# Attention of block 1: scores with the keys on partitions, and sums from a column of ones beside V

## The reference, cut to what matters

```python
def blocked_gqa(q, k, v):
    ...
    def one_block(qi):
        s = jnp.einsum("bqgrd,bkgd->bgrqk", qi, k)
        p = jax.nn.softmax(s, axis=-1)
        return jnp.einsum("bgrqk,bkgd->bqgrd", p, v)
```

## Time and profile before

| | |
|---|---|
| median of 3 runs | 2699.52 us (2699.20 to 2699.63) |
| span of the profiled execution | 2697.8 us |
| TensorE busy with matmuls | 2665.9 us (99%), 13860 records |
| TensorE loading stationary operands | 2195.1 us (81%) |
| DVE busy | 1526.9 us (57%) |
| ACT busy | 1173.5 us (43%) |

### The profile page before, as it was taken

One profiled execution on the slowest core, in us unless ns is written; L12 is line 12 of the kernel. 1 busy time (PEld: TensorE's weight loads), 2 busy tenths in 40 slices (PEclk: granted clock), 3 DMA queues, 4 the chain that ended last, 5 costly groups with the idle time before them and its releaser, 6 DMA issues.

```text
span 2697.8 us, 33846 instructions
## 1 busy us (share of the span) xinstructions
PE 2665.9 (99%) x13860; PEld 2195.1 (81%) x13860; DVE 1526.9 (57%) x2142; ACT 1173.5 (43%) x1732; POOL 26.8 (1%) x45
## 2 busy tenths in 40 slices
PE   9989999999989999999999999999999999999998
PEld 8777888888777888888888888888777888888887
DVE  7885444345885444344444356899978844544433
ACT  6784332225784322233322234455688452432221
POOL 0000000000000000000000000000000000000000
PEclk9999999999999999999999999999999999999999
DMA  6303333324303333333333342222223432333332
GB/s 216 94 2 110 100 96 95 98 83 148 94 2 110 102 94 97 97 94 97 100 94 96 98 138 86 72 74 76 77 86 96 133 94 94 98 98 94 98 94 67
DMA packets 75801, 255.55 MB, mean 95 GB/s; under 512 B 9088, under 2 KB 12288, under 8 KB 75264
## 3 DMA queue, kind: packets, MB, share of 16 engines
q1 hardware_dynamic: 73136, 240.29, 29.3%
q0 software_dynamic: 2512, 13.11, 1.3%
HBM read 241.30 MB, written 8.39 MB: 93 GB/s over the span
## 4 chain that ended last, share of the span: by engine, by line
PE 93%; DVE 4%; ACT 3%; issue 1%; DVEq 0%; ACTq 0%
PE PS L1469 27%; PE PS L1471 27%; PE PS L1470 27%; PE PS L1719 1%; PE PS L1701 1%; PE PS L1428 1%; PE PS L1488 1%; PE PS L1487 1%; PE PS L1489 1%; DVE WLO L2216 0%; PE PS L1665 0%; ACT WHI L1805 0%; PE PS L1537 0%; PE PS L1535 0%; PE PS L1539 0%
## 5 line engine op out<-in xcount | busy, mean ns | idle before, releaser
L1469 PE MATMUL PS<-HHI,WHI 128*128 128x512 f32 x2256 | 893.2, 396 | 0.0
L1471 PE MATMUL PS<-HHI,WLO 128*128 128x512 f32 x2256 | 878.8, 390 | 0.0
L1470 PE MATMUL PS<-HLO,WHI 128*128 128x512 f32 x2256 | 878.3, 389 | 0.0
L2216 DVE TENSOR_TENSOR WLO<-WR,WHI 128x1024 fp32r<-128x1024 f32 (+2 forms) x450 | 535.0, 1191 | 495.4 <-ACT WHI L1805 492.2
L1805 ACT CAST WHI<-WR 128x1024 fp32r<-128x1024 f32 (+2 forms) x450 | 457.5, 1018 | 445.6 <-PE PS L1471 421.9
L1469 PEld LDWEIGHTS PS<-HHI,WHI 128*128 128x128 f32 x2256 | 423.6, 188 | 92.1 <-issue 4.8
L1470 PEld LDWEIGHTS PS<-HLO,WHI 128*128 128x128 f32 x2256 | 423.7, 188 | 89.9 <-issue 4.1
L1471 PEld LDWEIGHTS PS<-HHI,WLO 128*128 128x128 f32 x2256 | 423.4, 188 | 88.8
L1469 PE MATMUL PS<-FHI,WHI 128*128 128x512 f32 x682 | 265.3, 389 | 0.0
L1470 PE MATMUL PS<-FLO,WHI 128*128 128x512 f32 x682 | 265.3, 389 | 0.0
L1471 PE MATMUL PS<-FHI,WLO 128*128 128x512 f32 x682 | 265.3, 389 | 0.0
(11 more groups left out here) (381 smaller groups left out, 2727.5 us busy)
## 6 DMA issues: line engine op xcount, KB each, us to landing
WR<-in_stream SPq DMA_DIRECT2D x402, 512.0 KB, 3.6
WR<-in_stream SPq DMA_DIRECT2D x32, 384.0 KB, 3.0
xkeep<-X POOLq DMA_DIRECT2D x3, 2048.0 KB, 9.4
X<-xkeep POOLq DMA_DIRECT2D x24, 256.0 KB, 4.7
WR<-in_stream SPq DMA_DIRECT2D x16, 328.0 KB, 4.0
ROT<-RQ SPq DMA_DIRECT2D x40, 64.0 KB, 2.0
X<-in_xin SPq DMA_DIRECT2D x8, 256.0 KB, 4.9
out<-X SPq DMA_DIRECT2D x8, 256.0 KB, 2.2
```

The costliest lines, as they stand in the source:

```text
L1469: e.matmul(out, hi[:, i, :], xhi, start=first, stop=False)
L1470: e.matmul(out, hi[:, i, :], xlo, start=False, stop=False)
L1471: t = e.matmul(out, lo[:, i, :], xhi, start=False, stop=final)
L2216: e.tensor_tensor(lo, raw, hi.bitcast(F32), ALU.subtract).then_inc(S["dve_low"], 1)
```

## The change

In each layer the attention is computed per head instead of per pair and chunk.
- **Maxima first.** `maxima` adds, for each pair m and each c, a step `qk` of two matmuls, one per head, on the 64 partitions that hold that head's high part (every fourth query, `c::CH`), against 64 partitions of `KDS[0]`. `max` reduces the result to the negated maximum, `NM`. No low part takes part, and nothing else is done with these scores.
- **The maximum as a row.** Per head two DMAs on SP's queue, `qdup` (the head's high part to `QM`, 64 rows) and `mrow` (the four columns of `NM` to row 64 of `QM`). On POOL two memsets write the ones: row 64 of `KDS[1]`, and column 64 of V's two groups.
- **Scores with keys on partitions.** `ks`, 4 steps per head: for 128 keys, `KDS[0]` stationary and the query tile moving, then `KDS[1]` (65 rows) stationary and `QM` moving: 512 queries along the free axis, the maximum already subtracted. `exp` writes the exponentials straight to a tile `PTS`; there is no `accum_out`, `nrm`, `prs`, `pT` or `pta`.
- **PV with the probabilities stationary.** `pv`, one step per head: for each chunk of 128 queries and each of 4 key blocks a single-precision matmul, 128x128 exponentials stationary, 65 moving columns of V (the last one gives the sum). `yn` (DVE) divides.
- **Back to channels.** `hT`, one step per pair: four PE transposes, then `yv` on whole tiles of 512.
- **Plan.** The pauses `pace1` and `pace2` become 0.1, and `TIMES` has new entries. `kdup` has three DMAs instead of four.

```diff
@@ -152,7 +152,7 @@
...
-    "qk": (("pe", 0.92),), "qhi": (("act", 0.76785),), "qlo": (("dve", 1.3),), "pT": (("pe", 0.45),), "pv": (("pe", 0.95),),
+    "qk": (("pe", 0.25),), "ks": (("pe", 0.46),), "mrow": (("sp", 0.3),), "qdup": (("sp", 0.1),), "qhi": (("act", 0.76785),), "qlo": (("dve", 1.3),), "hT": (("pe", 0.45),), "pv": (("pe", 1.9),),
...
+    "max": (("dve", 0.7),), "yn": (("dve", 0.75),), "yv": (("act", 0.62), ("dve", 0.7),),
...
+DELAY = {"v": 0.38043, "zsilu": 0.77358, "pace1": 0.1, "pace2": 0.1, "turned": 0.81963, "sums": 0.30369, "ss": 1.401,
+         "hsum": 0.075925, "picked": 0.55886, "lru": 5.6906, "sq": 0.27228, "third": 0.17664, "merged": 0.20081, "until": 0.087442, "row": 2.6}
@@ -198,8 +198,10 @@
-PR_OF = [i % 3 if i < 8 else (3, 4, 2, 0, 1)[(i - 8) % 5] for i in range(4 * NH)]
-PR_BEFORE = {i: max(k for k in range(i) if PR_OF[k] == PR_OF[i]) for i in range(4 * NH) if PR_OF[i] in PR_OF[:i]}
+TILES = NH * CH
+EARLY = 24
+PT_OF = [i % 5 if i < EARLY else (4, 5, 6, 7, 8, 0, 1, 2)[i - EARLY] for i in range(TILES)]
+PT_BEFORE = {i: max(k for k in range(i) if PT_OF[k] == PT_OF[i]) for i in range(TILES) if PT_OF[i] in PT_OF[:i]}
@@ -595,61 +597,68 @@
             yield from self.added(("rope", l, t - 1))
         self.add("rcs", l, t)
 
...
+    def maxima(self, l, m):
+
+        for c in range(CH):
+            yield from self.room(2)
+            while self.tokens_wait:
+                yield 0.1
+            for h in (2 * m, 2 * m + 1):
+                self.take(("qk", l, h, c), "side")
+            yield self.add("qk", l, m, c)
+            for h in (2 * m, 2 * m + 1):
+                last = self.add("max", l, h, c)
+                self.free(("qk", l, h, c), ("dve_max", last))
+            yield self.pace
+        yield last
+        for h in (2 * m, 2 * m + 1):
+            self.spawn(self.head(l, h))
+
+    def head(self, l, h):
+
+        if h > 0:
+            yield from self.added(("ks", l, h - 1, CH - 1))
+        if h >= 2:
+            yield from self.until(("ks", l, h - 2, CH - 1))
+        self.add("qdup", l, h)
+        self.add("mrow", l, h)
+        yield DELAY["row"]
+        for k in range(CH):
+            i = CH * h + k
+            if i in PT_BEFORE:
+                yield from self.added(("pv", l, PT_BEFORE[i] // CH))
+            if PT_OF[i] >= 5:
+                yield from self.added(("qlo", l, 4))
+            yield from self.room()
+            while self.tokens_wait:
+                yield 0.1
+            self.take(("ks", l, h, k), "side")
+            yield self.add("ks", l, h, k)
+            exp = self.add("exp", l, i)
+            self.free(("ks", l, h, k), ("act_exp", exp))
+            yield self.pace
         yield exp
...
+        if h > 0:
+            yield from self.added(("yn", l, h - 1))
         yield from self.room()
...
+        self.take(("pv", l, h), "side")
+        yield self.add("pv", l, h)
+        done = self.add("yn", l, h)
+        self.free(("pv", l, h), ("dve_yn", done))
+        if h % 2:
+            yield done
+            yield from self.room()
+            self.take(("hT", l, h // 2), "side")
+            yield self.add("hT", l, h // 2)
+            self.free(("hT", l, h // 2), ("dve_yv", self.add("yv", l, h // 2)))
 
     def attention(self, l):
         yield from self.until(("v", l))
...
+        for m in range(NH // 2):
+            yield from self.until(("kdup", l), ("qlo", l, 1 + m))
+            if m > 0:
+                yield from self.added(("qk", l, m - 1, CH - 1))
+            self.spawn(self.maxima(l, m))
 
     def conv(self, l, j):
         if j > 0:
@@ -1234,12 +1243,12 @@
-    V = sb("V", 192, [CH, P])
-    PR = sb("PR", 194, [2, T])
-    PT = sb("PT", 198, [2, 2, CH, P])
-    NM = sb("NM", 206, [8])
-    RSM = sb("RSM", 206.0625, [8])
-    RIN = sb("RIN", 206.125, [8])
+    V = sb("V", 192, [CH, 2, 65])
+    PT = sb("PT", 194.03125, [5, T])
+    QM = (sb("QM", 76, [T], F32R), sb("QM2", 204.03125, [T], F32R))
+    NM = sb("NM", 206.03125, [NH, CH], F32R)
+    RIN = sb("RIN", 206.1875, [2, CH])
+    YVS = (sb("YV", 180, [4, T]), sb("YV2", 207.5, [4, T]))
...
+    PTS = [PT[:, i, :] for i in range(5)] + [RQ[:, i, :] for i in range(4)]
@@ -1356,6 +1366,10 @@
+    def heads_tokens(m):
+        return YVS[m // 2][:, 2 * m % 4, :].rearrange("p (c x) -> p c x", c=CH)
@@ -1676,31 +1690,40 @@
                 transposes(step, [Z[:, c, i * P:(i + 1) * P] for c in range(CH)]).then_inc(S["pe_turn"], 1)
 
             elif kind == "qk":
...
+                l, m, c = a
+                q.wait_ge(s_keys, 48 * (l + 1))
                 q.wait_ge(S["dve_qlow"], n["qlo", l, 1 + m])
...
+                for i, half in enumerate((slice(0, 64), slice(64, P))):
+                    emptied(q, ("qk", l, 2 * m + i, c))
+                    t = e.matmul(PS[o.bank["qk", l, 2 * m + i, c]][:, :], query(2 * m + i)[half, c::CH],
+                                 KDS[0][half, m // 2, :], start=True, stop=True)
                 t.then_inc(S["pe_qk"], 1)
...
+            elif kind == "ks":
+                l, h, k = a
+                emptied(q, step)
+                q.wait_ge(S["pool_ones"], 2 * l + 2)
+                q.wait_ge(s_qm[h % 2], 32 * (4 * l + h // 2 + 1))
+                keys = slice(k * P, (k + 1) * P)
+                e.matmul(PS[o.bank[step]][:, :], KDS[0][:, h // 4, keys], query(h), start=True, stop=False)
+                e.matmul(PS[o.bank[step]][:, :], KDS[1][0:65, h // 4, keys], QM[h % 2][0:65, :], start=False, stop=True
+                         ).then_inc(S["pe_ks"], 1)
             elif kind == "pv":
...
+                l, h = a
+                out = PS[o.bank[step]]
                 emptied(q, step)
+                q.wait_ge(S["pool_ones"], 2 * l + 1)
                 q.wait_ge(S["act_v"], n["v", l])
...
+                q.wait_ge(S["act_exp"], n["exp", l, CH * h + CH - 1])
+                for c in range(CH):
+                    for k in range(CH):
+                        t = e.matmul(out[:, 65 * c:65 * c + 65], PTS[PT_OF[CH * h + k]][:, c * P:(c + 1) * P], V[:, k, h // 4, :],
+                                     start=k == 0, stop=k == CH - 1)
                 t.then_inc(S["pe_pv"], 1)
+            elif kind == "hT":
+                l, m = a
+                emptied(q, step)
+                q.wait_ge(S["dve_yn"], n["yn", l, 2 * m + 1])
+                transposes(step, [heads_tokens(m)[:, c, :] for c in range(CH)]).then_inc(S["pe_turn"], 1)
 
             elif kind == "lp":
                 j, k = a
@@ -1991,31 +2015,16 @@
 
             elif kind == "exp":
                 l, i = a
...
+                q.wait_ge(S["pe_ks"], n["ks", l, i // CH, i % CH])
+                if PT_OF[i] >= 5:
+                    q.wait_ge(S["dve_qlow"], n["qlo", l, 4])
+                if i in PT_BEFORE:
+                    q.wait_ge(S["pe_pv"], n["pv", l, PT_BEFORE[i] // CH])
+                e.activation(PTS[PT_OF[i]], PS[o.bank["ks", l, i // CH, i % CH]][:, :], ACT.Exp).then_inc(S["act_exp"], 1)
             elif kind == "yv":
...
+                l, m = a
+                q.wait_ge(S["pe_turn"], n["hT", l, m])
+                e.copy(YHI[:, m, :], PS[o.bank["hT", l, m]][:, :]).then_inc(S["act_yv"], 1)
 
             elif kind == "small":
                 q.wait_ge(S["dve_chain"], 5)
@@ -2486,22 +2495,20 @@
                                        ALU.mult, ALU.subtract).then_inc(S["dve_yz"], 1)
 
             elif kind == "max":
...
+                l, h, c = a
+                q.wait_ge(S["pe_qk"], n["qk", l, h // 2, c])
+                e.tensor_reduce(NM[:, h, c:c + 1], PS[o.bank["qk", l, h, c]][:, :], AX, ALU.max, negate=True).then_inc(S["dve_max"], 1)
+            elif kind == "yn":
+                l, h = a
+                got = PS[o.bank["pv", l, h]][:, 0:65 * CH].rearrange("p (c x) -> p c x", c=CH)
+                q.wait_ge(S["pe_pv"], n["pv", l, h])
+                settle(e.reciprocal(RIN[:, h % 2, :], got[:, :, 64]))
+                e.tensor_tensor(heads_tokens(h // 2)[:, :, 64 * (h % 2):64 * (h % 2) + 64], got[:, :, 0:64],
+                                RIN[:, h % 2, :].unsqueeze(2).to_broadcast([P, CH, 64]), ALU.mult).then_inc(S["dve_yn"], 1)
             elif kind == "yv":
...
+                l, m = a
+                q.wait_ge(S["act_yv"], n["yv", l, m])
+                e.tensor_tensor(YLO[:, m, :], PS[o.bank["hT", l, m]][:, :], YHI[:, m, :].bitcast(F32),
                                 ALU.subtract).then_inc(S["dve_yv"], 1)
 
             elif kind == "small":
@@ -2709,6 +2716,15 @@
+            elif kind == "v":
+                l, = a
+                done(q, ("z", l))
+                e.memset(V[:, :, :, 64:65], 1.0).then_inc(S["pool_ones"], 1)
+            elif kind == "kdup":
+                l, = a
+                q.wait_ge(s_keys, 48 * (l + 1))
+                q.wait_ge(S["pool_ones"], 2 * l + 1)
+                e.memset(KDS[1][64:65, :, :].bitcast(F32), 1.0).then_inc(S["pool_ones"], 1)
```

(15 more changed lines are left out.)

135 lines of the change are left out of this document (14 added, 121 removed).

## The result

The changed kernel takes **2722.6 us** (median of four runs, 2720.3 to 2724.6) against 2699.5 for the one before: ratio 1.0084, 95% interval 1.0069 to 1.0098, or +23.1 us. The forecast was 2706 with a range of 2691 to 2722: the sign of the likeliest case was right, the size was wrong by 16.6 us, and the result lies just above the range. The profiled execution has a span of 2718.5 us, 20.7 more than before. It is the fastest of the four: its mean granted clock is 0.997, and the two slowest (2723.5 and 2724.6 us) have 0.994.

A forecast was written before the change was run, and what follows sets the result against it. The prediction took TensorE's work plus about 9 us of waits per layer as the bound. Work +10.2 and recovered waits -7 gave +3.2 per layer, +6.4 for both: 2699.5 + 6.4 = 2706 us, range 2691 to 2722.

The forecast's parts named there:

- the likeliest case: Whole kernel: slower than before, 2700 to 2714 us, given a chance of 0.55.
- The prices: TensorE's work per layer: transposes -13.9 and +1.7, old pv -17.1, new pv +28.6, maxima +10.9, together +10.2 us.
- A visit: Two 64-row maxima matmuls side by side on TensorE: 0.68 us each, 16 per layer, +10.9 us.
- The weights' stride of four ... I take it at nothing: Maxima matmuls: loading every fourth query as weights was priced at zero, with the upper bound said to cover it.
- the old form: Old pv, two matmuls side by side: 17.1 us per layer go; the new pv's 28.6 was called 60% more.
- waits hidden under the records: TensorE's attention stretch: beyond at least 9.1 us of visible waits per layer, overlapping records hide more; 11.5 taken in all.
- The recovery: TensorE's waits in attention: of 11.5 us per layer 4.5 stay, so 7 us per layer are won back as ACT's work falls.
- The step that failed: SP's queue: 16 new DMAs per layer leave later loads 16 us to spare; mrow's 2.0 us or more hide under other work.
- The second half of the same step: TensorE's clock in the attention stretch: read as staying at 1.00, 2.4 GHz; no loss was priced.
- DVE or the row becomes the bound: Rival, chance 0.13: SSD is pushed behind attention, its DVE work stands alone, nothing is recovered; 2720 to 2730 us.
- long PE waits for `QM`'s DMA: Sign named beforehand that the forecast is wrong: TensorE standing long for the transfers into QM; no size given.
- Weight rows that wait for `WLO`: Sign named beforehand that the forecast is wrong: SP's or DVE's queue holds the weight loads up; no size given.

The follow-up runs named there:

- experiment 7: The changed kernel with 33 moving columns in place of 65 in each pv matmul, leaving out half of the attention's output columns: 2752.6 us.
- experiment 9: The changed kernel with 128 moving columns in place of 65 in each pv matmul, the surplus output ignored: 2722.1 us.
- experiment 4: The changed kernel without maxima, their row's transfers and the shift in the scores; exponentials of a scaled argument: 2701.4 us.
- experiment 1: The changed kernel with the qdup and mrow transfers issued by POOL in place of SP, nothing else changed: 2706.2 us.
- experiment 13: The changed kernel with TensorE kept busy by unused matmuls while it waits for the row ahead of heads 0 and 1: 2715.7 us.
- experiment 8: The changed kernel, row left in SP's queue, its order planned with the row's delay and corrected swap, transfer, pv and visit times: 2718.6 us.

## Why the prediction was wrong

**The prices were right, their sum can't be seen whole.** `pv` 3.57 against 3.6 us a head; it is bound by the load (experiments 7 and 9: 33, 65 and 128 columns all take 3.49). `ks` starts 0.455 us apart in pairs, as `qk` did. `hT` 0.36 to 0.59. A visit is 0.75 among rows against 0.68, but 0.40 where two stand together, and 0.66 in the mean of experiment 4. "The weights' stride of four ... I take it at nothing" was wrong by 0.12 us a visit. (The new `pv` costs 67% more than the old form, 28.6 / 17.1, and not 60%; the sum has the right terms.) TensorE's busy time rose by 21.4 us (2665.9 to 2687.3); less the 6.8 at half speed that is 14.6, or 7.3 per layer where the sum has +10.2. The 2.4 us per layer that the forecast took for waits hidden under the records would count as busy time before the change and make up most of the difference, but no row shows them.

**The recovery was right as far as ACT's waits go.** They ended. Experiment 1, which has the forecast's work and no wait for the row, takes 2706.2 us, and the forecast was 2706. That agreement is better than its parts. TensorE's idle time (span less busy) is 22.1 us there against 31.9 before, 9.8 less where 2 x 7 = 14 were forecast, and its busy time 16.1 more, of which at most 1.7 is clock, where 20.4 were forecast. The two misses cancel; either the hidden 2.4 us stand on both sides, or it is luck.

**The step that failed** is the last of the part on waits: "SP's queue gets 16 DMAs per layer, each behind a wait ... with three slots, 16 us, to spare. `mrow` itself takes at least the 2.0 us of a swap, under rows or another head's `pv`". I asked what the new transfers do to those behind them, and that slack held: no weight row waited for its load. I didn't ask what stands ahead of the new transfers. There a swap waits 6 us for ACT's `raw` and then takes 2.4 us to issue, and TensorE, in order, stood 3.6 to 4.0 us for head 0 and 0.9 for head 1 of each layer, 9.4 us in all, where the forecast had put the row under other work. So of the recovery of 14 us only 0.7 came (idle 31.9 to 31.2 us). Taking the wait away gave back 9.0 us of idle time (experiment 1), of the 16.6 by which the forecast was off.

**The second half of the same step** is a price the prediction doesn't have: the clock. It was read once, as 1.00 in the earlier trace rows, and taken as given. It fell in three stretches behind waits; 6.8 us (experiment 13). The kernel before has more idle time in this stretch, 9.1 us per layer, in a dozen pieces of 1.7 us at most, and its clock never falls there; here 9.0 us of waiting for the row cost 15.8. A sum of idle microseconds isn't a price. Why one wait is followed by a fall and the next is not stays open: the 2.0 us wait before `run` was followed by one in layer 1 of the changed kernel and by none in its layer 2.

**The rival that had the size** ("DVE or the row becomes the bound", 0.13, 2720 to 2730) had the row in its name, and its mechanism is another: SSD pushed behind attention. That didn't happen in the changed kernel, so it is luck that its range holds the result: nearly nothing of the waits was recovered, as it has it, but because of the row. It did when the maxima were taken away (experiment 4), which no part of the prediction had foreseen. Of the signs named beforehand, "long PE waits for `QM`'s DMA" was the one to be seen. "Weight rows that wait for `WLO`" is there too, 1.3 us before the first output rows against 0.65 before.

**Open** is why the last convolution of DVE is 2.0 to 2.4 us late before `run` in every version but those of experiments 4 and 8, and whether a `pv` in the old form (V as weights, two heads side by side, 17.1 in place of 28.6 us) can be had with the new scores: the sums would need tiles of their own, and it wasn't tried. Of the versions that were measured none beats the kernel before; the best one can't be told from it.

## What to carry to other kernels

For each transfer that a change adds, read the queue ahead of it as well as behind it: an in-order queue whose head waits for another engine holds up everything in it, while here the queue of an engine that was idle (POOL) took the same transfers at no cost that shows. Price a wait of TensorE by its length in one piece and by what follows it at which clock, not by the sum of idle time; and take work off the engine that bounds a stretch only after asking what that work had hidden.
